# Moving the causal mask of the attention scores from VectorE's shift tile to a TensorE matmul

## The reference

```python
logits = einsum('nqhd,nkhd->nhqk', q, k) * (FA_HEAD_DIM ** -0.5)
decay  = c_q[..., :, None] - c_k[..., None, :]      # running sums of log-forget values
causal = k_pos[None, :] <= q_pos[:, None]
logits = where(causal, logits + decay, -inf)
p      = softmax(logits)
o      = einsum('nhqk,nkhd->nqhd', p, v)            # then (o * silu(z)) @ w_out, and a LayerNorm
```

## Time and profile before

| | |
|---|---|
| time, median of 3 runs | 1877.4 us (1877.33 to 1881.37) |
| the profiled execution's own time | 1877.4 us |
| its span, first to last instruction | 1875.9 us |
| mean granted TensorE clock | 0.953 |
| PE, busy share of the span | 92% |
| DVE, busy share | 53% |
| ACT, POOL, busy share | 34%, 22% |
| instructions | 27945 |

### The profile page before, as it was taken

One profiled execution on the slowest core, in us unless ns is written; L12 is line 12 of the kernel. 1 busy time (PEld: TensorE's weight loads), 2 busy tenths in 40 slices (PEclk: granted clock), 3 DMA queues, 4 the chain that ended last, 5 costly groups with the idle time before them and its releaser, 6 DMA issues.

```text
span 1875.9 us, 27945 instructions
## 1 busy us (share of the span) xinstructions
PE 1731.6 (92%) x10128; PEld 1512.3 (81%) x10128; DVE 1002.7 (53%) x1523; ACT 637.1 (34%) x987; POOL 412.3 (22%) x424
## 2 busy tenths in 40 slices
PE   5999999999999969998699999999999998769866
PEld 2999999999999969998577878888888887447632
DVE  6433353333434362255516567666667576689763
ACT  5212222121111252244323636445454536342120
POOL 0000011110111000012212433425251524354130
PEclk8999999999999989999699999999999999779977
DMA  8111022222212213344122121112112032328493
GB/s 329 46 45 45 34 90 69 78 89 78 79 67 89 80 35 104 102 131 135 58 86 81 41 87 46 67 45 78 56 56 78 34 89 60 100 92 294 159 382 134
DMA packets 50190, 180.42 MB, mean 96 GB/s; under 512 B 6522, under 2 KB 8186, under 8 KB 48850
## 3 DMA queue, kind: packets, MB, share of 16 engines
q1 hardware_dynamic: 32802, 120.30, 18.9%
q0 software_dynamic: 17328, 59.33, 9.0%
HBM read 154.07 MB, written 17.15 MB: 91 GB/s over the span
## 4 chain that ended last, share of the span: by engine, by line
PE 73%; DVE 12%; issue 5%; ACT 5%; DMA 3%; POOL 1%; POOLq 0%; DVEq 0%; SPq 0%; ACTq 0%
PE bank L1645 18%; PE bank L1647 18%; PE bank L1646 18%; PE bank L1812 2%; PE bank L1882 2%; DMA pages<-cache_v 2%; PE bank L1749 2%; PE bank L1931 2%; PE bank L1913 1%; PE bank L1912 1%; DVE pages L1353 1%; PE bank L1933 1%; PE bank L1932 1%; POOL p_lo L529 1%; PE bank L1729 1%
## 5 line engine op out<-in xcount | busy, mean ns | idle before, releaser
L1645 PE MATMUL bank<-h_hi,w_lo 128*128 128x344 f32 x1152 | 373.6, 324 | 0.8 <-DVE w_lo L1009 0.5
L1646 PE MATMUL bank<-h_lo,w_hi 128*128 128x344 f32 x1152 | 367.7, 319 | 0.0
L1647 PE MATMUL bank<-h_hi,w_hi 128*128 128x344 f32 x1152 | 367.5, 319 | 0.0
L529 POOL TENSOR_TENSOR p_lo<-parg,p_hi 128x512 fp32r<-128x512 f32 (+1 forms) x192 | 210.1, 1110 | 191.0 <-ACT p_hi L899 189.2
L1645 PE MATMUL bank<-x_hi,w_lo 128*128 128x512 f32 x528 | 222.4, 421 | 8.7 <-POOL x_lo L486 6.4
L1645 PEld LDWEIGHTS bank<-h_hi,w_lo 128*128 128x128 f32 x1152 | 216.8, 188 | 4.9 <-issue 3.5
L1646 PEld LDWEIGHTS bank<-h_lo,w_hi 128*128 128x128 f32 x1152 | 216.7, 188 | 0.5 <-issue 0.5
L1647 PEld LDWEIGHTS bank<-h_hi,w_hi 128*128 128x128 f32 x1152 | 216.5, 188 | 0.0
L1646 PE MATMUL bank<-x_lo,w_hi 128*128 128x512 f32 x528 | 213.2, 404 | 0.0
L1647 PE MATMUL bank<-x_hi,w_hi 128*128 128x512 f32 x528 | 213.0, 403 | 0.0
L1645 PE MATMUL bank<-y_hi,w_lo 128*128 128x320 f32 (+2 forms) x512 | 178.4, 348 | 26.1 <-ACT y_hi L720 9.4
(11 more groups left out here) (299 smaller groups left out, 2810.9 us busy)
## 6 DMA issues: line engine op xcount, KB each, us to landing
raw<-units SPq DMA_DIRECT2D x121, 512.0 KB, 3.3
ada_ring<-w_ada SPq DMA_DIRECT2D x32, 512.0 KB, 3.3
pages<-cache_k POOLq DMA_DIRECT2D x32, 512.0 KB, 5.3
pages<-cache_v POOLq DMA_DIRECT2D x32, 512.0 KB, 16.4
ada_first<-w_ada SPq DMA_DIRECT2D x8, 1024.0 KB, 12.0
ckb<-scr_c POOLq DMA_DIRECT2D x16, 512.0 KB, 4.6
KX<-KA SPq DMA_DIRECT2D x32, 256.0 KB, 4.2
scr_x<-x1f POOLq DMA_DIRECT2D x8, 512.0 KB, 3.8
```

The costliest lines, as they stand in the source:

```text
L529: g.tensor_tensor(p_lo[:, r, off:HALF], parg[:, r, off:HALF], p_hi[:, r, off:HALF].bitcast(F32), ALU.subtract).then_inc(S("p_ready"), 1)
L1645: mm(out, lhs_lo, rhs_hi, start=first, stop=False)
L1646: mm(out, lhs_hi, rhs_lo, start=False, stop=False)
L1647: return mm(out, lhs_hi, rhs_hi, start=False, stop=last)
```

## The change

`maskb` is built transposed (the other triangle). `peak` swaps the two operands of its mask matmul, so that its result is the same as before. `scores` adds the mask itself: in the eight diagonal chunks each head gets a third matmul, `maskb` with `identb`, over the first 128 columns of its output, and the semaphore `s_done` is raised by that one. `mask_block` and the waits on `mb_masked` are gone from DVE; `mb` stays as ACT wrote it.

```diff
             g.affine_select(out=maskb[:, :], in_=maskb[:, :], compare_op=ALU.is_gt, fill=0.0, base=0,
-                            pattern=[[-1, P]], channel_multiplier=1).then_inc(S("consts"), 1)
+                            pattern=[[1, P]], channel_multiplier=-1).then_inc(S("consts"), 1)
...
-            def mask_block(j, c):
-
-                half, kt, off, slot, diag = chunk(c)
-                if kt == 0:
-                    dve.wait_ge(S("mb_ready"), 2 * j + 1)
-                else:
-                    dve.wait_ge(S("arg_ready"), 24 * j + 2 * c)
-                v.tensor_tensor(mb[:, :, off:off + P], mb[:, :, off:off + P], over(maskb[:, :], 2), ALU.add)\
-                    .then_inc(S("mb_masked"), 1)
-
             def exponents(j, c):
                 half, kt, off, slot, diag = chunk(c)
-                if c == 0:
-                    mask_block(j, 0)
-                if diag:
-                    dve.wait_ge(S("mb_masked"), 8 * j + kt + 1)
                 for h in range(2):
...
-                if c in (0, 1, 2, 7, 8, 9, 10):
-                    mask_block(j, c + 1)
...
-                    mm(out[:, qs], maskb[:, :], identb[:, :], start=False, stop=True).then_inc(S("m_done"), 1)
+                    mm(out[:, qs], identb[:, :], maskb[:, :], start=False, stop=True).then_inc(S("m_done"), 1)
...
                     mm(out, KA[:, h, ks], QA[:, h, qs], start=True, stop=False)
-                    last = mm(out, KX[:, h, ks], QA[:, h, qs], start=False, stop=True)
+                    last = mm(out, KX[:, h, ks], QA[:, h, qs], start=False, stop=not diag)
+                    if diag:
+                        last = mm(out[:, 0:P], maskb[:, :], identb[:, :], start=False, stop=True)
                     last.then_inc(S("s_done"), 1)
```

## The result

The change made the kernel slower, by more than I had forecast. The median is 1894.2 us over 4 runs (1883.4 to 1896.6) against 1879.4 us for the kernel before (4 runs, 1877.3 to 1883.3). The two medians alone would give a ratio of 1.0079; the measured ratio, for which eight executions of the changed kernel are listed (1883.4 to 1896.6), is 1.0064, interval 1.0035 to 1.0094. I had forecast 1884.4 us and a range to 1889. The profiled execution took 1887.8 us, its span is 1886.2 us and its mean granted clock 0.958.

What follows compares the result with a forecast made beforehand. PE, busy 92% of the span, was taken to bound pairs 0 to 6, with DVE's list mattering in the last pair; +7.9 and -0.9 made +7.0 us, from 1877.4 to 1884.4 us, range 1878 to 1889.

Steps and rivals of the forecast that it cites:

- The price of a mask: Added PE matmuls in scores: 0.125 us per wide mask, 0.08 per narrow, 1.82 us a head pair, 12.7 for seven.
- Rival 1: Masks in scores nearly free at 0.04 us each, leaving only the last pair's gain: 1876.5 us; chance 0.22.
- The turn to the next pair: PE's wait at the next pair's first token product takes back 0.3 us, seven times: 2.1 us.
- the one on what is removed: DVE's mask additions in pairs 0 to 6 count at nothing, covered by its wait for PE.
- the one on the waits: PE's wait at values of chunk 0 soaks up 0.42 us in six pairs, 0.2 in pair 0: 2.7 us.
- rival 4: A stretch of PE products falls from full to half clock rate, costing 3 us: 1887; chance 0.05.
- The sum for seven pairs: Pairs 0 to 6: 12.7 us of added masks less 2.7 and 2.1 taken back by waits, net +7.9 us.
- The last pair: Fewer DVE additions from chunks 7 to 11 gain 1.0 us, limited by PE, less 0.07: -0.9 us.
- a sign of being wrong: Named beforehand for the changed kernel's profile: the last head pair gaining more than 2 us.
- rival 3: Last pair faster because DVE's mask additions no longer slow POOL's p_lo: 1871.3 us; chance 0.04.
- Rival 2: PE's waits in the seven pairs soak up nothing: 12.7 us less 0.9, 1889.2 us; chance 0.10.

Runs made afterwards that it cites:

- dve_half: Changed kernel without the mask matmuls in the scores, so the causal mask within the diagonal tiles is left out; 1881.2 us, ratio 1.0022.
- early: Changed kernel with DVE's split of the next pair's Q weights moved ahead of the exponents of chunk 1; 1880.1 us, ratio 1.0016.
- swap_pe: Changed kernel with PE's scores of chunk 2 ahead of the values of chunk 0; 1880.7 us, ratio 1.0012.
- pe_half: Kernel before with the mask matmuls added in the scores and DVE's mask additions kept; 1886.2 us, ratio 1.0046.
- before_early: Kernel before with DVE's split of the next pair's Q weights moved ahead of the exponents of chunk 1; 1882.0 us, ratio 1.0023.
- one_left: Changed kernel with only DVE's mask addition for chunk 2 left, just ahead of the split, and all mask matmuls kept; 1893.6 us, ratio 1.0081.
- again: Changed kernel run once more, nothing altered; 1894.1 us, ratio 1.0091 to the kernel before.
- hybrid: Kernel before, with only the last head pair taking its masks from PE instead of DVE; 1873.2 us, ratio 0.9979.
- early_paired: early, with both heads' masks behind one another in chunks 1, 2, 3, 8 and 9; 1881.0 us, ratio 1.0014.

## Why the prediction was wrong

- **The price of a mask** was right. From the first scores product of the middle pair to the last product with the values it cost 2.19 us, of which 0.35 is the grown wait: 1.84 us a pair for 16 matmuls, against 1.82 predicted. Rival 1 is out.
- **The turn to the next pair** was right: it gives 0.33 us back, against 0.3.
- **The failed step** is the one on what is removed, and the one on the waits that rests on it: "In the seven phases I count them at nothing, since the wait for PE covers them. ... None is ahead of a PE wait that I can see", and then "0.42 us, all of it soaked up". I looked at what depends on an addition and not at what stands behind it in DVE's list. That is the split, which PE doesn't need just then, but it reads and writes SBUF beside POOL's subtraction. Without the addition it starts 0.37 us earlier, ahead of the subtraction instead of behind it. The term was -2.7 us; in its place PE loses 0.77 us in six pairs less the 0.42 it had lost, and 0.60 less 0.22 in pair 0: +2.5. `dve_half`, `early` and `swap_pe` show it from three sides, and the two orders within `pe_half` agree.
- **The clock** was rival 4, at 0.05. In the changed kernel the early stretches added 3.1 us, in one pair or two. All the traces with early stretches have PE standing for some time shortly before them: the three of the changed kernel (a loss of 0.77), `dve_half` (1.2), `before_early` (0.20 + 0.80) and `one_left` (0.6, at `w_lo`). None of the eight others has one, with losses up to 0.5. But their number doesn't follow the loss: `one_left`, with the smallest, has six, `dve_half`, with the largest, has one, and in the changed kernel most pairs have the loss and no stretch. I take the wait as one condition for them; that is read from which kernels have them, and no run changed the clock alone.
- **The sum for seven pairs**: 12.9 for the masks, + 2.5, - 2.3 for the turns, + 3.1 for the clock = 16.2 us, and 613.4 - 597.2 is 16.2. Predicted were 7.9. (Two small things cancel in it: the stretches at the turns, 0.9 us, are missing after, and pair 6 grows by 0.8 more than the others.)
- **The last pair** gained 2.4 us and not 0.9, more than the 2 us that I had named as a sign of being wrong. The gain is that of the DVE half: the stretch takes 48.3 us in `dve_half` and 51.1 in `pe_half`. The term let PE limit it to 1.0 us; in the changed kernel DVE waits only 0.07 us for scores on its way from the exponents of chunk 7 to those of chunk 11, and takes 14.75 us for it instead of 17.46. The four additions make up 1.4 of this. A collision that was mine to see makes up 1.1: before, DVE's product of pages and query (line 1353) started 0.04 us behind POOL's subtraction at 1651.27, and took 2.30 us; now it is out of step with it. DVE's timeline of the kernel before, then of the changed one:

```profile
1651.31 2.30 DVE L1353 TENSOR_TENSOR pages<-pages,qb 128x1024 f32<-128x1024 f32 x1
...
1664.49 1.22 DVE L1353 TENSOR_TENSOR pages<-pages,qb 128x1024 f32<-128x1024 f32 x1
1665.74 1.22 DVE L1356 TENSOR_REDUCE scol<-pages 128x16 f32<-128x1024 f32 x1
```

 The other side is that DVE comes to chunk 7 0.3 us later than before. So rival 3 had the mechanism, DVE against POOL, and half of its place: here the change takes DVE out of POOL's way, and in the seven other pairs it puts it there.
- **What is left.** Pairs and last pair make 16.2 - 2.4 = 13.8 us. The profiled spans differ by 10.3, because the attention started 2.8 us sooner in this execution (1017.4 against 1020.2) and the rest was 0.6 shorter. The timed medians of `again` differ by 16.6. The remaining 3 us are not assigned. In the three profiled executions of the changed kernel the pairs take the same time, and what differs is the start, by 0.9 us, and the end, by 6.5, which is longer where the clock is lower; the slowest executions were not profiled. What sets these is open.
- Rival 2's total, 1889.2, was nearer than my own, for another reason: its matmuls were to be hidden by nothing, and `pe_half` shows that they are hidden as I had said.

## What to carry to other kernels

When an instruction is taken out of an engine's list, look at what moves up behind it, and what that meets on another engine: a DVE instruction with two SBUF inputs and a POOL instruction that works on SBUF took turns here like users of one shared resource, and a few hundredths of a microsecond decided which of them waited and so whether PE did. Try each half of a move alone, and try it phase by phase: this change loses in the seven pairs where PE is full and gains in the one where DVE is (`hybrid`, 0.2%), and only there is it worth making.

## What the runs showed of the hardware

- **DVE and POOL took turns on SBUF, whole instructions at a time, where DVE's had two SBUF inputs.** POOL's subtraction of 512 columns takes 1.3 us alone and 2.26 behind a DVE split of 1.31; the split takes 1.22 alone and 2.31 behind a subtraction; an addition of 256 columns takes 0.43 alone and 1.52. The one that started first is hardly slowed. DVE's exponent line, with one input in PSUM, ran beside POOL's subtraction at no cost to either: at 384 columns it takes 0.61 us with and without it in `early`, and the subtraction 1.29 us beside exponent lines only and 1.30 alone. The Trainium skill ("Trainium Architecture — The Big Picture", What this means for kernel authors) calls the port pair that the two engines share an exclusive lock and not a split of bandwidth; these durations agree.
- **A short matmul's cost falls mostly on the product behind its follower**, 0.32 us from start to start instead of 0.23. Two masks behind one another cost about 0.07 us less than two apart (2.5 us less in seven pairs with five chunks each so arranged, in `early_paired`).
- **Half-clock stretches within a pair in which PE is busy throughout**: those of 3.4 us (clock 0.55) cost 1.5 us each and those of 6.8 us (clock 0.53) 3.1, and where they fell, and how many there were, differed between executions of the same kernel. They came only a few microseconds behind a stand of PE of 0.6 to 1.2 us; that the stand brings them on is not shown.
